# The last stage before attention in a hybrid encoder kernel: another order for the router's product, another buffer for the last q rows, earlier loads of w_out

## The chip, the cores and the metric

The kernel runs on one core of one Trainium2 chip. The metric is the device time of one execution in microseconds (us), median of several runs. Engines are named PE (matmul; PEld is its weight load), DVE, ACT, POOL and SP; SPq and ACTq are the DMA queues that SP and ACT issue on.

## The reference, cut to what matters

Two sequences of 1024 tokens go through one encoder layer: layer norm, a mixer of grouped-query attention and a two-directional RG-LRU, a second layer norm and a hierarchical mixture of experts. Around the change it computes:

```python
proj = h @ w_in                                   # q, k, v, x_lru, y_lru
q = apply_axial_rope(rms_norm(q, q_norm_g), ...)  # the same for k
lru = (h_fwd + h_bwd) * gelu(y_lru)
merged = concatenate([rms_norm(attn, attn_out_g), rms_norm(lru, lru_out_g)])
mix = merged @ w_out
h = layer_norm(DEEPNORM_ALPHA * h + mix, ln1_g, ln1_b)
g_logits = h @ router_wg                          # and e_logits = h @ router_we
```

The kernel reaches the router's logits partly through a product `w_out @ r_w`, where `r_w` holds the 20 columns of `router_wg` and `router_we`. That product needs `w_out` transposed on PE, and it is made in the stage that this case is about.

## The kernel before

`build` calls the stages one after the other: `project_xy`, `qkv_lru`, `attend`, `route`, `experts`, `combine`. Each is a block of its own, and a stage starts when all engines have ended the one before. The change is inside `qkv_lru`.

`qkv_lru` has two interleaved jobs. **Tiles**: for each of 16 tiles of 128 tokens (NT = 16), `front(t)` on PE projects h onto q, k, v and the router's columns with three matmul passes into PSUM tile `pj[t % 2]`; ACT's `square(t)` reads it; DVE and POOL normalise and rotate it; ACT's and POOL's `split(t)` make high and low parts in `q_st` and `k_st`; `back(t, uses)` on PE transposes them into `tr` (uses 0 and 1 are q, use 2 is k); ACT's `evict_q(t)` copies q into the one buffer `q_t`, and `evict_k(t)` issues the store of `q_t` to `q_dram` and copies k. `evict_q(t)` waits until the store of tile t - 1 has landed (`q_stored`). The profile calls `q_t` and its neighbours `wq_raw`, since they lie in that room. **LRU units**: 8 units (NU = 8) of gates, decays, scans and outputs; ACT's `squares_of_output(n)` squares unit n's output and PE's `sums(n, ...)` adds the squares up with matmuls of one column. `GROUPS` gives the order: tile 0, then pairs (1, 2) to (13, 14), then tile 15 alone, which is group g = NU.

The third job is the product with the router's columns. It has UNITS_W = 16 **steps**, and a step n is three things: `turn_w(n)`, four transposes of 128x128 of `w_out` into `gp[n % 2]` (L921); `read_w(n)` on ACT, which copies them to `wo_t[n % 2]` (L1064, shown as `w_out_rows<-gp`); and `times_w(n)`, which multiplies them with `r_w` into `pj[0]` (L930). On PE `times_w(n)` is followed by `turn_w(n + 2)`. `read_w(n)` waits for `turn_w(n)` and `times_w(n - 2)`. After steps 7 and 15 `read_r(half)` copies the product to `lru_th` and `turn_r(half)` transposes it back into `pj[1]`; the last ACT instruction of the stage copies `pj[1]` to `w_r` (shown as `w_out_router<-pj`, L1158).

`w_out` comes in five loads on SP's queue, `WO_LOADS`: rows of 128 numbered (0, 1), (1, 2), (2, 4), (4, 6), (6, 8). The first two, 512 KB each, go to room left by `c_hi` and `c_lo`; the other three, 1024 KB each, go to `wo_late` (shown as `ln_in_g_b`) and are issued once `front(15)` is done.

In the code before, group g = NU places steps 0 to 3 around the transposes of tiles 13 and 14, and then all other steps behind them.

## Time and profile before

| | us |
|---|---|
| median of 3 runs | 1619.41 |
| lowest and highest of them | 1618.01, 1620.03 |
| the profiled execution's own time | 1620.24 |
| its span, first to last instruction | 1618.5 |

The mean granted TensorE clock over the span is 0.956 of full speed, and PE is busy for 90% of it. In what follows times are in us from the start of the span. The stage `qkv_lru` ends near 498.6 and `attend` starts with its first instructions near 499.7. A row of a timeline gives start, duration, engine, line, operation, output and input, the number of instructions merged, and in brackets the idle time before it and what ended it. Rows of matmuls overlap, since matmuls are pipelined: from one row's start to the next is the time that the engine spent on it.

### The profile page before, as it was taken

Reading aid. Unit: us, or ns where it says so; the run is one execution under the profiler, and the core shown is the slowest. Engines: PE = TensorE matmul, PEld = TensorE weight load, DVE = VectorE, ACT = ScalarE, POOL = GpSimd, SP = SyncE. Lnnn points to the kernel's source line nnn. Section 1 sums busy time; section 2 is a strip of 40 time slices with the busy share of each in tenths; the row PEclk is TensorE's granted clock in tenths of the full one; section 3 lists DMA queues with packets and bytes.
Section 4 is the critical chain, followed back from the end, with each engine's and each line's share of the span. In section 5 each row is a group of like instructions: output and inputs, shape, how many; then the busy total and the mean of one; then the engine's idle time right before and its main releaser. Section 6 shows DMA issues by size and latency. Waiting matters only on the chain. (4 is left out here: it accounts for less than half of the span.)

```text
span 1618.5 us, 30220 instructions
## 1 busy us (share of the span) xinstructions
PE 1449.3 (90%) x8946; PEld 1261.0 (78%) x8947; DVE 1125.9 (70%) x2208; ACT 927.7 (57%) x1625; POOL 483.4 (30%) x345
## 2 busy tenths in 40 slices
PE   5999989999976899999999999973999999999940
PEld 5999977777754899999999999972777788777820
DVE  8787548999955888888888888877444333444237
ACT  3444338787855766666666666632555544556325
POOL 1212124575520011111121111122454534544218
PEclk9999999999988999999999999995899999999975
DMA  8865542534444112211112221126798787796576
GB/s 286 303 226 200 211 145 86 189 144 173 165 147 138 61 39 93 72 65 59 59 60 80 76 78 59 47 97 198 233 270 263 182 248 207 200 273 164 104 224 257
DMA packets 126214, 250.09 MB, mean 155 GB/s; under 512 B 24498, under 2 KB 77746, under 8 KB 126132
## 3 DMA queue, kind: packets, MB, share of 16 engines
q1 hardware_dynamic: 94000, 160.97, 28.7%
q0 software_dynamic: 12528, 45.99, 12.3%
q10 hardware_dynamic: 19604, 42.09, 6.8%
q8 instruction: 45, 0.74, 0.2%
q14 instruction: 37, 0.30, 0.1%
HBM read 154.35 MB, written 94.67 MB: 154 GB/s over the span
## 5 line engine op out<-in xcount | busy, mean ns | idle before, releaser
L1736 DVE TENSOR_TENSOR d_probs_t_lo<-d_pt_ps,d_probs_t_hi 128x512 fp32r<-128x512 f32 x256 | 164.9, 686 | 63.4 <-ACT d_probs_t_hi L1650 61.8
L1914 POOL TENSOR_TENSOR d_h_tile<-d_s_tile,d_ln_g_b 128x512 f32<-128x512 f32 x30 | 38.9, 1296 | 532.3 <-ACT d_s_tile L1683 514.6
L1650 ACT ACTIVATE d_probs_t_hi<-d_pt_ps 128x512 fp32r<-128x512 f32 x256 | 139.2, 596 | 95.9 <-PE d_pt_ps L1531 89.5
L1712 DVE TENSOR_REDUCE d_neg_max<-d_s_ps 128x1 f32<-128x1024 f32 x128 | 155.6, 1215 | 3.5 <-PE d_s_ps L1520 3.5
L121 PE MATMUL acc<-k_hi,wl_hi 128*128 128x256 f32 x512 | 145.2, 284 | 4.5 <-DVE k_lo L576 4.5
L121 PE MATMUL e_a_ps<-up_hi,e_xt_hi 128*128 x336 | 136.6, 406 | 10.8 <-issue 5.5
L1633 ACT ACTIVATE d_probs<-d_s_ps,d_neg_max 128x1024 f32<-128x1024 f32 x128 | 143.5, 1121 | 4.2 <-DVE d_neg_max L1712 4.2
L122 PE MATMUL acc<-k_lo,wl_hi 128*128 128x256 f32 x512 | 144.3, 282 | 0.0
L123 PE MATMUL acc<-k_hi,wl_lo 128*128 128x256 f32 x512 | 144.3, 282 | 0.0
L1531 PE MATMUL d_pt_ps<-ident,d_probs 128*128 128x128 f32 x1024 | 132.9, 273 | 4.7 <-ACT d_probs L1633 3.2
L1545 PE MATMUL d_ot_ps<-d_probs_t_hi,d_v_split 128*128 128x256 f32 x512 | 127.4, 287 | 8.3 <-DVE d_probs_t_lo L1736 8.3
L123 PE MATMUL e_a_ps<-up_hi,e_xt_lo 128*128 x336 | 132.5, 394 | 0.0
L122 PE MATMUL e_a_ps<-up_lo,e_xt_hi 128*128 x336 | 132.1, 393 | 0.0
L1545 PE MATMUL d_ot_ps<-d_probs_t_lo,d_v_split 128*128 128x256 f32 x512 | 124.9, 282 | 0.0
L1531 PEld LDWEIGHTS d_pt_ps<-ident,d_probs 128*128 128x128 f32 x1024 | 116.9, 140 | 7.7 <-ACT d_probs L1633 6.5
L121 PE MATMUL d_m_ps<-d_wo_hi,d_m_hi 128*128 128x348 f32 x360 | 120.6, 335 | 0.0
L1519 PE MATMUL d_s_ps<-k_hi,d_q_tile 128*128 128x512 f32 (+1 forms) x256 | 112.0, 438 | 5.7 <-DMA d_q_tile<-q_dram 5.7
L122 PE MATMUL d_m_ps<-d_wo_lo,d_m_hi 128*128 128x348 f32 x360 | 115.8, 322 | 0.0
L123 PE MATMUL d_m_ps<-d_wo_hi,d_m_lo 128*128 128x348 f32 x360 | 115.5, 321 | 0.0
L2391 POOL DMA_INDIRECT e_xg<-h_dram,e_ix x45 | 45.1, 1003 | 231.1 <-ACT e_yt L2518 124.9
L1545 PEld LDWEIGHTS d_ot_ps<-d_probs_t_hi,d_v_split 128*128 128x128 f32 x512 | 97.2, 190 | 15.4 <-issue 15.4
L121 PEld LDWEIGHTS acc<-k_hi,wl_hi 128*128 128x128 f32 x512 | 97.8, 191 | 5.1 <-DVE k_lo L576 5.1
(405 smaller groups left out, 4079.2 us busy)
## 6 DMA issues: line engine op xcount, KB each, us to landing
up_raw<-in_exp_w SPq DMA_DIRECT2D x32, 1024.0 KB, 13.0
down_raw<-in_exp_w SPq DMA_DIRECT2D x16, 1024.0 KB, 13.0
d_h_tile<-h_dram SPq DMA_DIRECT2D x16, 522.0 KB, 4.7
h_dram<-v_all ACTq DMA_DIRECT2D x16, 512.0 KB
ht_hi_dram<-k_hi ACTq DMA_DIRECT2D x8, 1024.0 KB, 4.3
ht_lo_dram<-k_lo ACTq DMA_DIRECT2D x8, 1024.0 KB, 6.7
q_dram<-wq_raw ACTq DMA_DIRECT2D x16, 512.0 KB, 3.0
d_q_tile<-q_dram SPq DMA_DIRECT2D x16, 512.0 KB, 4.2
```

The costliest lines, as they stand in the source:

```text
L121: pe.matmul(out, lhs[0], rhs[0], start=first, stop=False)
L122: pe.matmul(out, lhs[0], rhs[1], start=False, stop=False)
L123: return pe.matmul(out, lhs[1], rhs[0], start=False, stop=last)
L1519: pe.matmul(out, q_t[u][:, h, :], k_hi[:, h // GQ, keys], start=True, stop=False)
L1531: last = pe.transpose(pt_ps[c][:, j, :], pr[h % 2][:, k * P:(k + 1) * P], ident[:])
L1545: last = pe.matmul(ot_ps[:, 0:2 * P], vs[:, s * TPS + k, h // GQ].rearrange("p c d -> p (c d)"), part[:, k].rearrange("p e t -> p (e t)"), ...
L1633: act.activation(pr[h % 2][:], s_ps[h % 2][:], ACT.Exp, bias=nm[:, u, h:h + 1], accum_out=rsum[:, u, h:h + 1]).then_inc(p_done, 1)
L1650: act.activation(pt_hi[:, c * HALF:(c + 1) * HALF, h % 2], pt_ps[c][:], ACT.Copy).then_inc(pth_done[c], 1)
L1712: dve.tensor_reduce(nm[:, u, h:h + 1], s_ps[h % 2][:], AX, ALU.max, negate=True).then_inc(nm_done, 1)
L1736: dve.tensor_tensor(pt_lo[:, part, h % 2], pt_ps[c][:], pt_hi[:, part, h % 2].bitcast(F32), ALU.subtract)\
L1914: pool.tensor_tensor(h1[:, part], s_t[u][:, part], g_b[:, part], ALU.mult).then_inc(hg_done, 1)
L2391: pool.indirect_dma_start(xg[u][:], None, h1_dram, bass.IndirectOffsetOnAxis(ix[u][:, 0:1], 0))\
```

## The change

Steps are placed by number: group NU now holds only `front(15)`, after which PE runs all sixteen steps in a row. Between them come the transposes of tile 13 (q after step 3, k after step 4), of tile 14 (after 6 and 7) and of tile 15 (after 12 and 13), the sums of unit 6 (after step 5, formerly inside `front(15)`) and of unit 7 (after step 14), and `turn_r(0)` after step 9. ACT's list of instructions is rewritten to match. For tile 15 `evict_q` writes to `q_st[0]`, and not to `q_t`, and waits for no store. The load of rows 2 and 3 of `w_out` goes to the gates' weights' room (`gw`, shown as `gate_w`) once the last gate matmul is done; the loads of rows 4 to 7 go ahead of the load of y for unit 7 on SP's queue. The sums of units 6 and 7 are copied by one instruction instead of two.

```diff
--- before.py
+++ after.py
@@ -739,6 +739,7 @@
         tab = both_rt[:, 0:TPS * 2 * HD].rearrange("p (t c d) -> p t c d", t=TPS, c=2)
         q_t = room(NQ * P).bitcast(F32R).rearrange("p (h t) -> p h t", h=NQ)
         q_st = [sb(f"q_st{u}", [P, NQ, 2, HD], F32R) for u in range(2)]
+        q_rows = lambda t: q_t if t < NT - 1 else q_st[NT % 2][:].rearrange("p h c d -> p h (c d)")
 
         gw = sb("gate_w", [P, FT, NG, P])
         ones = sb("ones_b", [P, 2])
@@ -756,7 +757,8 @@
         hr_done = sem("h_router_done")
         hr_stored = sem("h_router_stored")
         wo_early = [c_room[:, n * D:(n + 1) * D] for n in range(4)]
-        wo = wo_early[0::2] + [wo_late[:, k * D:(k + 1) * D] for k in range(KD - 2)]
+        wo_gates = gw[:].rearrange("p f g n -> p (f g n)")
+        wo = wo_early[0::2] + [wo_gates[:, k * D:(k + 1) * D] for k in range(2)] + [wo_late[:, k * D:(k + 1) * D] for k in range(KD - 4)]
         wo_t = wo_early[1::2]
         WO_LOADS = ((0, 1), (1, 2), (2, 4), (4, 6), (6, KD))
         UNITS_W = 2 * KD
@@ -860,14 +862,26 @@
                     load_x(g + 1)
                 if 2 * g + 2 < NT:
                     load_c(2 * g + 2)
-                if g >= NU - 1:
-                    rows = w_out[0].rearrange("(k p) n -> p k n", p=P)
+                rows = w_out[0].rearrange("(k p) n -> p k n", p=P)
+                if g == NU - 1:
                     for n, (a, b) in enumerate(WO_LOADS):
-                        if (b <= 2) != (g == NU - 1):
+                        if b <= 2:
+                            sp.wait_ge(pj_done, NT - 1)
+                            dst = wo[a]
+                        elif b <= 4:
+                            sp.wait_ge(gates_done, GH * NU)
+                            dst = wo_gates[:, (a - 2) * D:(b - 2) * D]
+                        else:
                             continue
-                        sp.wait_ge(pj_done, NT - 1 if b <= 2 else NT)
-                        dst = wo[a] if b <= 2 else wo_late[:, (a - 2) * D:(b - 2) * D]
                         sp.dma_start(dst.rearrange("p (k n) -> p k n", n=D), rows[:, a:b, :]).then_inc(wo_in[n], 16)
+                    store(NU - 2)
+                    sp.wait_ge(pj_done, NT)
+                    for n, (a, b) in enumerate(WO_LOADS):
+                        if a >= 4:
+                            sp.dma_start(wo_late[:, (a - 4) * D:(b - 4) * D].rearrange("p (k n) -> p k n", n=D), rows[:, a:b, :])\
+                              .then_inc(wo_in[n], 16)
+                    load_y(NU - 1)
+                    continue
                 if g == NU:
                     sp.wait_ge(hr_done, NT)
                     with nc.allow_non_contiguous_dma("the router's columns of h's rows"):
@@ -881,11 +895,11 @@
         @block.tensor
         def _(pe):
 
-            def sums(n, out):
+            def sums(n, out, first=SUMS):
                 pe.wait_ge(ones_made, 1)
                 pe.wait_ge(squared, n + 1)
                 for c in range(TPS):
-                    last = pe.matmul(out[:, SUMS + c:SUMS + c + 1], r[n % 2][:, 1, c * P:(c + 1) * P], ones[:, 0:1],
+                    last = pe.matmul(out[:, first + c:first + c + 1], r[n % 2][:, 1, c * P:(c + 1) * P], ones[:, 0:1],
                                      start=True, stop=True)
                 return last
 
@@ -899,9 +913,6 @@
                     for k in range(KD):
                         last = three_pass(pe, pj[u][:, a:b], (c[0][:, k, :], c[1][:, k, :]),
                                           (w_hi[:, k, a:b], w_lo[:, k, a:b]), k == 0, k == KD - 1)
-                if t == NT - 1:
-                    turn_w(0)
-                    turn_w(1)
                 if unit is not None:
                     last = sums(unit, pj[u])
                 last.then_inc(pj_done, 1)
@@ -970,38 +981,33 @@
             for g, group in enumerate(GROUPS):
                 turned = GROUPS[g - 1] if g else []
                 for t in group:
-                    front(t, g - 2 if g >= 2 and t == group[-1] else None)
+                    front(t, g - 2 if 2 <= g < NU and t == group[-1] else None)
                 if g == NU:
-                    for n in range(2):
-                        times_w(n)
-                        turn_w(n + 2)
+                    continue
                 for half in range(2):
                     if half < len(turned):
                         back(turned[half], (0, 1))
-                    if g < NU:
-                        gates(g, 2 * half)
+                    gates(g, 2 * half)
                     if half < len(turned):
                         back(turned[half], (2,))
-                    if g < NU:
-                        gates(g, 2 * half + 1)
-                    if g == NU and half == 0:
-                        times_w(2)
-                        times_w(3)
-            turn_w(4)
-            turn_w(5)
-            for n in range(4, 10):
-                times_w(n)
-                turn_w(n + 2)
-            back(NT - 1, (0, 1, 2))
-            turn_r(0)
-            for n in range(10, 12):
-                times_w(n)
-                turn_w(n + 2)
-            sums(NU - 1, pj[1]).then_inc(last_sums, 1)
-            for n in range(12, UNITS_W):
+                    gates(g, 2 * half + 1)
+            turn_w(0)
+            turn_w(1)
+            for n in range(UNITS_W):
                 times_w(n)
                 if n + 2 < UNITS_W:
                     turn_w(n + 2)
+                if n in (3, 6, 12):
+                    back(NT - 3 + (3, 6, 12).index(n), (0, 1))
+                if n in (4, 7, 13):
+                    back(NT - 3 + (4, 7, 13).index(n), (2,))
+                if n == 5:
+                    pe.wait_ge(v_done, NT)
+                    sums(NU - 2, pj[1]).then_inc(last_sums, 1)
+                if n == 9:
+                    turn_r(0)
+                if n == 14:
+                    sums(NU - 1, pj[1], SUMS + TPS).then_inc(last_sums, 1)
             turn_r(1)
 
         @block.scalar
@@ -1040,16 +1046,16 @@
                    .then_inc(hi_done, 1)
 
             def evict_q(t):
-                if t:
+                if 0 < t < NT - 1:
                     act.wait_ge(q_stored, 16 * t)
                 for part in range(2):
                     use = 3 * t + part
                     act.wait_ge(tr_done, use + 1)
-                    act.activation(q_t[:, 4 * part:4 * part + 4], tr[use % 2][:].bitcast(F32), ACT.Copy).then_inc(tr_free, 1)
+                    act.activation(q_rows(t)[:, 4 * part:4 * part + 4], tr[use % 2][:].bitcast(F32), ACT.Copy).then_inc(tr_free, 1)
 
             def evict_k(t):
                 act.wait_ge(tr_free, 3 * t + 2)
-                act.dma_start(q_dram[TILES[t]], q_t.rearrange("p h t -> p (h t)").bitcast(F32)).then_inc(q_stored, 16)
+                act.dma_start(q_dram[TILES[t]], q_rows(t).rearrange("p h t -> p (h t)").bitcast(F32)).then_inc(q_stored, 16)
                 use = 3 * t + 2
                 act.wait_ge(tr_done, use + 1)
                 cols = slice(TILES[t] * P, (TILES[t] + 1) * P)
@@ -1104,55 +1110,58 @@
             def root(n):
                 act.activation(th[:], th[:], ACT.Sqrt, scale=0.25).then_inc(root_done, 1)
 
-            for g, group in enumerate(GROUPS):
+            for g, group in enumerate(GROUPS[:NU]):
                 turned = GROUPS[g - 1] if g else []
-                if g in (1, NU):
+                if g == 1:
                     split(turned[0])
-                if g == NU:
-                    read_w(0)
-                    read_w(1)
-                square(group[0], g - 2 if g == NU else None)
-                if g < NU:
-                    tanh_table()
+                square(group[0])
+                tanh_table()
                 if len(turned) > 1:
                     split(turned[1])
-                if g == NU:
-                    read_w(2)
-                    read_w(3)
                 if len(group) > 1:
                     square(group[1], g - 2 if g >= 2 else None)
                 for half in range(2):
                     if half < len(turned):
                         evict_q(turned[half])
-                    if g < NU:
-                        gate_tanhs(g, 2 * half)
+                    gate_tanhs(g, 2 * half)
                     if half < len(turned):
                         evict_k(turned[half])
-                    if g < NU:
-                        gate_tanhs(g, 2 * half + 1)
-                if g < NU:
-                    decays(g)
+                    gate_tanhs(g, 2 * half + 1)
+                decays(g)
                 if 0 < g < NU - 1:
                     split(group[0])
-                if g < NU:
-                    root(g)
-                if 0 < g < NU:
+                root(g)
+                if 0 < g < NU - 1:
                     squares_of_output(g - 1)
+            read_w(0)
+            read_w(1)
+            split(NT - 3)
+            square(NT - 1)
+            read_w(2)
+            split(NT - 2)
+            read_w(3)
+            squares_of_output(NU - 2)
             read_w(4)
             read_w(5)
+            evict_q(NT - 3)
+            read_w(6)
+            evict_k(NT - 3)
+            read_w(7)
+            read_w(8)
+            evict_q(NT - 2)
+            read_w(9)
+            evict_k(NT - 2)
+            read_w(10)
+            read_r(0)
             split(NT - 1)
-            for n in range(6, 12):
+            for n in range(11, 15):
                 read_w(n)
-            read_r(0)
             evict_q(NT - 1)
+            read_w(15)
             evict_k(NT - 1)
-            read_w(12)
-            read_w(13)
             squares_of_output(NU - 1)
-            read_w(14)
-            read_w(15)
-            act.wait_ge(last_sums, 1)
-            keep_sums(NU - 1, 1)
+            act.wait_ge(last_sums, 2)
+            act.activation(lru_sums[:, NU - 2:NU, :], pj[1][:, SUMS:SUMS + 2 * TPS].rearrange("p (n c) -> p n c", c=TPS), ACT.Copy)
             read_r(1)
             act.wait_ge(wr_turned, 2)
             act.activation(w_r[:], pj[1][:, 0:KD * RW].rearrange("p (k r) -> p k r", k=KD), ACT.Copy)
```

On PE, from the last matmul of `front(15)`, before the change (L921 is `turn_w`, L888 `sums`, L930 `times_w`, L955 `back`; "x4" are four instructions):

```order
L123 MATMUL pj<-wq_hi,c_lo 128x276
L921 MATMUL gp<-ident,w_out_rows 128x128 x8
L888 MATMUL pj<-ones_b,lru_r 128x1 x8
L930 MATMUL pj<-w_out_rows,logits 20x256 x2
L921 MATMUL gp<-ident,w_out_rows 128x128 x4
L930 MATMUL pj<-w_out_rows,logits 20x256 x2
L921 MATMUL gp<-ident,w_out_rows 128x128 x4
L955 MATMUL tr<-identr,q_st 128x128 x8
L955 MATMUL tr<-identr,k_st 128x128 x4
L930 MATMUL pj<-w_out_rows,logits 20x256 x4
L955 MATMUL tr<-identr,q_st 128x128 x8
L955 MATMUL tr<-identr,k_st 128x128 x4
```

And after the change, from `turn_w(4)`, the first one that reads `gate_w`, to the sums of unit 6 (L932 is `turn_w`, L941 `times_w`, L966 `back`, L902 `sums`):

```order
L932 MATMUL gp<-ident,gate_w 128x128 x4
L941 MATMUL pj<-w_out_rows,logits 20x256 x2
L932 MATMUL gp<-ident,gate_w 128x128 x4
L966 MATMUL tr<-identr,q_st 128x128 x8
L941 MATMUL pj<-w_out_rows,logits 20x256 x2
L932 MATMUL gp<-ident,gate_w 128x128 x4
L966 MATMUL tr<-identr,k_st 128x128 x4
L941 MATMUL pj<-w_out_rows,logits 20x256 x2
L932 MATMUL gp<-ident,gate_w 128x128 x4
L902 MATMUL pj<-ones_b,lru_r 128x1 x8
```

The transposes of tiles 13 and 14 stood together after step 3's transposes; now each half of a tile stands behind a `times_w` and a `turn_w` of its own.

On ACT, the end of the stage before the change (L1048 is `evict_q`, L1052 and the two rows behind it `evict_k`, L1015 `squares_of_output`, L1011 the copy of the sums, L1070 `read_r`):

```order
L1048 ACTIVATE wq_raw<-tr 128x512 x2
L1052 DMA q_dram<-wq_raw 128x1024
L1056 ACTIVATE k_hi<-tr 128x2x128
L1057 ACTIVATE k_lo<-tr 128x2x128
L1064 ACTIVATE w_out_rows<-gp 128x512 x2
L1015 ACTIVATE lru_r<-lru_y 128x1024
L1064 ACTIVATE w_out_rows<-gp 128x512 x2
L1011 ACTIVATE lru_sums<-pj 128x8
L1070 ACTIVATE lru_th<-pj 20x512
L1158 ACTIVATE w_out_router<-pj 128x160
```

And after it (L1054 is `evict_q` of tile 15, which now writes `q_st`, L1070 `read_w`, L1021 `squares_of_output`, L1076 `read_r`):

```order
L1054 ACTIVATE q_st<-tr 128x512 x2
L1070 ACTIVATE w_out_rows<-gp 128x512
L1058 DMA q_dram<-q_st 128x1024
L1062 ACTIVATE k_hi<-tr 128x2x128
L1063 ACTIVATE k_lo<-tr 128x2x128
L1021 ACTIVATE lru_r<-lru_y 128x1024
L1164 ACTIVATE lru_sums<-pj 128x16
L1076 ACTIVATE lru_th<-pj 20x512
L1167 ACTIVATE w_out_router<-pj 128x160
```

The squares of unit 7 stand behind the last `read_w` and the last tile's copies, where two `read_w` stood behind them before.

## Rows read from the trace of the kernel before

**Rows 1.** Stretches of the stage: busy time and count of each engine, PEclk, DMA.

```profile
460.40:473.50 13.10, 5.84 (x29) 3.94 (x28) 10.34 (x11) 3.76 (x8) 3.51 (x5) 0.61 0.68 220
473.50:487.00 13.50, 12.50 (x74) 6.59 (x72) 0.00 (x0) 6.26 (x12) 0.96 (x2) 1.00 0.16 64
```

**Rows 2.** PE's waits, 450.3 to 499: total, times, longest.

```profile
PE tr L955 <- ACT wq_raw L1048: 8.8, 3, 7.3
```

**Rows 3.** PE's timeline over the same stretch.

```profile
450.30 1.03 PE L921 MATMUL gp<-ident,w_out_rows 128*128 128x128 f32 x8
451.59 1.92 PE L888 MATMUL pj<-ones_b,lru_r 128*128 128x1 f32 x16 [0.26 <-ACT lru_r L1015]
453.44 1.04 PE L930 MATMUL pj<-w_out_rows,logits 128*20 128x256 f32 x4
...
468.53 0.72 PE L955 MATMUL tr<-identr,k_st 128*128 128x128 f32 x4 [7.26 <-ACT wq_raw L1048]
469.05 1.93 PE L921 MATMUL gp<-ident,ln_in_g_b 128*128 128x128 f32 x8
470.91 1.90 PE L930 MATMUL pj<-w_out_rows,logits 128*20 128x256 f32 x4
...
473.58 1.04 PE L930 MATMUL pj<-w_out_rows,logits 128*20 128x256 f32 x4
474.55 0.66 PE L921 MATMUL gp<-ident,ln_in_g_b 128*128 128x128 f32 x4
475.14 1.04 PE L930 MATMUL pj<-w_out_rows,logits 128*20 128x256 f32 x4
...
488.79 2.10 PE L888 MATMUL pj<-ones_b,lru_r 128*128 128x1 f32 x16 [1.72 <-ACT lru_r L1015]
490.82 1.89 PE L930 MATMUL pj<-w_out_rows,logits 128*20 128x256 f32 x4
...
494.69 0.66 PE L921 MATMUL gp<-ident,ln_in_g_b 128*128 128x128 f32 x4
...
497.86 0.42 PE L940 MATMUL pj<-ident,lru_th 20*128 20x20 f32 x4 [0.68 <-ACT lru_th L1070]
```

**Rows 4.** ACT's timeline over the same stretch.

```profile
452.18 1.06 ACT L1064 ACTIVATE w_out_rows<-gp 128x512 f32<-128x512 f32 x2
453.54 0.70 ACT L1022 ACTIVATE wq_raw<-pj 128x640 f32<-128x640 f32 x1 [0.31 <-PE pj L888]
...
455.01 0.66 ACT L1038 ACTIVATE q_st<-wq_raw 128x512 fp32r<-128x512 f32 x1
...
455.83 0.63 ACT L1064 ACTIVATE w_out_rows<-gp 128x512 f32<-128x512 f32 x1
...
467.79 1.08 ACT L1048 ACTIVATE wq_raw<-tr 128x512 fp32r<-128x512 f32 x2 [8.25 <-DMA q_dram<-wq_raw]
...
484.19 0.38 ACT L1057 ACTIVATE k_lo<-tr 128x256 fp32r<-128x256 f32 x1
...
487.60 1.05 ACT L1015 ACTIVATE lru_r<-lru_y 128x1024 f32<-128x1024 f32 x1
...
498.31 0.30 ACT L1158 ACTIVATE w_out_router<-pj 128x160 f32<-128x160 f32 x1 [0.51 <-PE pj L940]
```

**Rows 5.** SP's queue, timeline 425 to 515: the DMAs it issues.

```profile
453.54 1.42 SPq L870 DMA_DIRECT2D ln_in_g_b<-in_w_out  x3
455.02 0.88 SPq L874 DMA_DIRECT2D h_dram<-h_router  x1
472.22 0.36 SPq L840 DMA_DIRECT2D lru_dram<-lru_y  x1
```

**Rows 6.** DMA issues with KB each and median us to landing, three stretches: 458 to 459, 468 to 484, 451 to 470.

```profile
q_dram<-wq_raw ACTq DMA_DIRECT2D x1, 512.0 KB, 9.3
...
q_dram<-wq_raw ACTq DMA_DIRECT2D x2, 512.0 KB, 2.6
...
h_dram<-h_router SPq DMA_DIRECT2D x1, 160.0 KB, 15.3
```

**Rows 7.** The three late loads of w_out (tile ln_in_g_b): time to landing.

```profile
DMA to landing us min/median/max: 6.5/9.5/14.4
```

## The prediction

> **What bounds the kernel now.** I first looked at the grouped stretches of the stage, because the page's average (PE busy 90%) says nothing about the 48 us between `front(15)` and the end of the stage. From 460.4 to 473.5 PE is busy for 5.84 of 13.1 us at a granted clock of 0.61, and from 473.5 to 487.0 for 12.5 of 13.5 us at 1.00 [rows 1]. So the same kind of work runs once with PE as the limit and once not. Then PE's waits: 8.8 us for ACT's L1048, `evict_q`, in three waits, of which one holds 7.3 us [rows 2]. Then the timelines. PE stops after tile 14's q transposes until 468.53, idle 7.26 us [rows 3]. ACT stood still at the same time, 8.25 us, and what ended its wait was a DMA, the store of tile 13's q rows [rows 4]. That store took 9.3 us to land, against 2.6 us for the next two [rows 6]. It left in the middle of the three late loads of `w_out`, issued at 453.54, the last of which needed 14.4 us [rows 5, 7]. The bound of the stretch is thus a chain: loads slow the store, the store holds `q_t`, ACT waits with `evict_q(14)`, PE waits with `back(14)`, and steps 4 to 15, though they need none of it, are queued behind on both engines. The stage's last instruction starts on ACT at 498.31 [rows 4].
>
> The chain matters one for one. `attend` begins when the stage has ended, and DVE and SP have long finished: unit 7's output is done by 472.22, when its store is issued [rows 5].
>
> **What PE loses in this stretch.** From 450.30, where the first transposes start, to 497.86, where the last four do, there are 47.6 us [rows 3].
> - Idle: 8.8 us on `evict_q` [rows 2], 0.26 and 1.72 us before the two `sums`, 0.68 us before the last `turn_r` [rows 3]. Sum 11.5.
> - A slow clock. At full clock one `times_w` takes 474.55 - 473.58 = 0.97 us and one `turn_w` 475.14 - 474.55 = 0.59, so a step is 1.56. From 469.05 to 473.58 PE did three `turn_w` and one `times_w` in 4.53 us where 3 x 0.59 + 0.97 = 2.74 would do: 1.8 lost. From 488.79 to 494.69 it did one `sums` (1.85, from 451.59 to 453.44), two `times_w` and one `turn_w` in 5.90, where 4.38 would do: 1.5 lost. Sum 3.3 [rows 3].
>
> Together 14.8 us that are not work at full speed. The work itself, sixteen steps, two sums, three tiles of transposes, two `turn_r`, is the same before and after: the `sums(6)` that leaves `front(15)` comes back after step 5, and one copy of eight columns less is off PE's path.
>
> **What the new order loses instead.** I put the new sequence of both engines side by side from 450.3 on with the durations above. Handing over costs about 0.03 us from a matmul's end to ACT. From ACT's end to PE I take 0.15, an estimate from 497.86, where 0.68 idle contains little but `read_r`. A `read_w` takes 0.6, its successor may start after 0.5 (two take 1.06) [rows 4].
> - Start: `read_w(0)` begins only after `turn_w(0)`, at 450.99, so `times_w(0)` starts at 451.74 where PE is free at 451.48. Idle 0.26.
> - `read_w(2)` stands behind two `read_w`, `split(13)` and `square(15)`. A `split` is 455.83 - 455.01 = 0.82, a `square` 455.01 - 453.54 = 1.47 with the copy of sums that now goes [rows 4]. ACT comes to `read_w(2)` at 454.3, it ends at 454.9, and PE, free at 454.86, starts `times_w(2)` at about 455.1. Idle 0.2.
> - From then on PE gives ACT 1.56 us for each step, and `read_w` needs 0.5 of it. One `split` (0.82), one `squares` (1.05) or one half of `evict_q` (1.08 for two) fits in, the more so as PE has transposes of its own in the same steps. I find no idle time to step 14.
> - `sums(7)` waits for `squares_of_output(7)`, which ACT now reaches only after `read_w(15)` and `evict_k(15)`. After `turn_w(15)` PE has left the k transposes (some 0.4) and `times_w(14)` (0.97), 1.3 us. ACT has 0.03 + 0.5 + two k copies (0.38 each, overlapping, 0.6 to 0.7) + 1.05 + 0.15, that is 2.4 [rows 4]. Idle 1.1.
> - The tail after `times_w(15)` is what it was, 0.68.
>
> Sum 2.2 us. By this schedule `evict_q(14)` starts at 466.6, `turn_w(8)`, the first that needs rows 4 and 5 of `w_out`, at 465.2, and the last ACT instruction near 486.
>
> **The clock.** Before, an idle time of 1.72 us and the `sums` of one column behind it were followed by matmuls at half speed: `times_w` took 1.90 at 490.82 against 1.04 [rows 3]. At 451.59 only 0.26 idle stood before the same `sums`, and the next `times_w` took 1.04. The new 1.1 lies between. I take the worse row: it costs `times_w(15)` 0.85 and the last `turn_r` some 0.15, so 1.0 us. The bound below is nothing.
>
> **DMAs and what they cost.** The load of rows 2 and 3 can go once the gates are done. PE does them ahead of `front(15)`, which ends at 450.3, and `turn_w(4)` needs the rows at 456.0: 5.7 us and the whole length of `front(15)`, where the first late load took 6.5. Rows 4 to 7 leave at about 450.6 instead of 454; with 14.4 us, the longest seen, the last byte is there at 465.0, just before `turn_w(8)` and 8 us before `turn_w(12)` [rows 7]. Store of unit 6 and load of y move behind those issues (about 0.5 us each, three took 1.42 [rows 5]) on SP's queue. y is needed by DVE near 471, and leaves at about 457.6, when `squares_of_output(6)` has run; nothing queued behind it (the router's columns of h, the last LRU store) is read before `attend`. In all 2048 + 512 + 160 KB then leave between 450.6 and 458.5. Before, 3072 + 512 + 512 + 160 = 4256 KB took from 453.54 to 455.02 + 15.3 = 470.3, some 253 KB per us, so they are through at about 461.4 [rows 5, 6]. Tile 13's store leaves at about 461.1, and should land in 2.6 to 4 us. `evict_q(14)` wants it at 466.6, and PE has 0.7 us of slack more: a landing within 6.2 us costs nothing. The other buffer for tile 15 saves nothing by itself, since tile 14's store would have 8 us anyway; I cost it at 0. Its own store leaves near 479.4 and even with 3 us lands before 486.
>
> **Sum.** 14.8 - 2.2 - 1.0 = 11.6 us off 1620.24, the profiled execution's own time: 1608.6. That execution was 0.83 above the median of the runs, so the predicted median is 1619.41 - 11.6 = 1607.8.
>
> **Rivals.**
> *The store still lands late.* y, the router's columns and the ends of `w_out` could still be in flight at 461. For it speaks the 9.3 us [rows 6]; against it that only a sixth as much is outstanding. With 9.3 us it lands at 470.4, `evict_q(14)` begins 3.8 us late and PE loses 3.1. After such a gap the clock would fall as after 468.53, 1.8 more. Gain 11.6 - 4.9 = 6.7: 1612.7.
> *Steps in a row lower the clock, and the kernel is slower.* More than a third of each step is transposes. Should the clock stay at its lower level through them, a step takes 473.58 - 470.91 = 2.67 instead of 1.56, and sixteen cost 17.8 more [rows 3]. The small idle times mostly vanish then, and the result is 1619.41 - 14.8 + 17.8 + 1.5 (sums, tile transposes, tail) = 1623.9. It decides against the change once about 11 of the 16 steps run so. Against it stands the stretch from 473.5 to 487.0, the same mix of steps, at clock 1.00 [rows 1]. The Trainium skill speaks for it: its page "TensorE: Matmul & The Clock Gate", Part 4 (PE-mode transpose), says that transposes don't count as busy for the clock as matmuls do. By that rule alone the time would be this rival's; the trace of this stage doesn't agree, as its clock rose and stayed up with both kinds in turn.
> *The stage's end is set elsewhere, no change.* SP waits for the router's columns of h. They would have to land 25 us later than the 473.4 that issue at about 458 and 15.3 us give [rows 6].
>
> **How the numbers follow.** Chances: forecast 0.78, late store 0.14, slow clock 0.03, no change 0.02, 0.03 for something in between or later. The likeliest case's own range: without a fall of the clock and with `sums` somewhat shorter the gain is 13; another 1 us either way can come from when the clock rises at the start of `attend`, whose first matmuls run after an idle time in both kernels. That gives 1605.5 below. Above, small waits at the many handovers, 0.1 us at each of some 20, and that 1 us give 1610.8. To leave out no more than 2 in 10, the range must take in most of the late store: up to 1612.7. A measurement of this kernel can tell about 0.2%, 3.2 us, from no change. Faster 0.93, within 0.03, slower 0.04.
>
> **What would show it.** Right: no wait of ACT on `q_dram` over 1 us in the stage; PE's idle time between `front(15)` and the last `turn_r` near 2 us, half of it before `sums(7)`; steps 1.56 us apart but where transposes of a tile come between; `w_out_router` at about 486.5; `attend`'s first instructions 1.1 to 1.4 us behind it as before. Wrong: a `turn_w` that waits for a load, an ACT wait before `evict_q(14)`, or PEclk at 0.5 within the steps.

## The result and the profile after

The changed kernel takes 1607.6 us (median of 7 runs, 1603.63 to 1614.01); the kernel before took 1621.95 in 7 runs (1618.01 to 1627.2). The ratio is 0.9908, 95% interval 0.9891 to 0.9926. The predicted median was 1607.8. The profiled execution took 1609.71 with a span of 1607.9, against 1620.24 before.

PE's timeline of the changed kernel, which answers to [rows 3]:

```profile
451.48 1.03 PE L932 MATMUL gp<-ident,w_out_rows 128*128 128x128 f32 x8
452.76 1.04 PE L941 MATMUL pj<-w_out_rows,logits 128*20 128x256 f32 x4 [0.25 <-ACT w_out_rows L1070]
...
455.29 0.66 PE L932 MATMUL gp<-ident,w_out_rows 128*128 128x128 f32 x4
456.00 1.04 PE L941 MATMUL pj<-w_out_rows,logits 128*20 128x256 f32 x4
...
467.99 0.66 PE L932 MATMUL gp<-ident,ln_in_g_b 128*128 128x128 f32 x4
468.40 0.54 PE L966 MATMUL tr<-identr,k_st 128*128 128x128 f32 x4
468.87 1.04 PE L941 MATMUL pj<-w_out_rows,logits 128*20 128x256 f32 x4
469.84 0.66 PE L932 MATMUL gp<-ident,ln_in_g_b 128*128 128x128 f32 x4
470.43 1.04 PE L941 MATMUL pj<-w_out_rows,logits 128*20 128x256 f32 x4
...
481.54 1.92 PE L902 MATMUL pj<-ones_b,lru_r 128*128 128x1 f32 x16 [1.01 <-ACT lru_r L1021]
483.38 1.78 PE L941 MATMUL pj<-w_out_rows,logits 128*20 128x256 f32 x4
485.84 0.61 PE L951 MATMUL pj<-ident,lru_th 20*128 20x20 f32 x4 [0.68 <-ACT lru_th L1076]
```

The 7.26 us before the k transposes of tile 14 are gone: that row, at 468.40, has no bracket. The steps behind it are 1.56 us apart (468.87 to 470.43). The three idle times that are left are 0.25, 1.01 and 0.68; the prediction had 0.26, 1.1 and 0.68, and 0.2 at `times_w(2)`. That one shows no bracket, but `times_w(2)` at 456.00 starts 0.71 us behind `turn_w(3)` where other steps have 0.59, so some 0.1 us of it is there. The kernel before had such a short wait without a bracket too, 0.77 us from a `turn_w` to tile 13's q transposes, where 0.41 would do (467.99 to 468.40 above):

```profile
455.97 0.66 PE L921 MATMUL gp<-ident,w_out_rows 128*128 128x128 f32 x4
456.74 0.88 PE L955 MATMUL tr<-identr,q_st 128*128 128x128 f32 x8
```

The `times_w` at 483.38 takes 1.78 and not 1.04.

Three stretches of the changed kernel, in the columns of [rows 1]:

```profile
451.48:480.50 29.02, 28.72 (x182) 16.93 (x180) 19.66 (x24) 19.16 (x42) 11.06 (x10) 1.00 0.51 157
480.50:483.40 2.90, 1.89 (x18) 1.88 (x18) 0.00 (x0) 0.89 (x1) 0.00 (x0) 1.00 0.31 127
483.40:487.00 3.60, 2.37 (x9) 0.91 (x8) 0.00 (x0) 1.07 (x3) 0.00 (x0) 0.52 0.00 0
```

PE is busy for 28.72 of 29.02 us at a clock of 1.00, through fifteen steps, three tiles' transposes and one `sums`. Only behind `sums(7)` does the clock fall, to 0.52 over the last stretch.

ACT's timeline of the changed kernel around its two critical places ([rows 4] before):

```profile
461.42 0.34 ACTq L1058 DMA_DIRECT2D q_dram<-wq_raw  x1
...
466.99 1.08 ACT L1054 ACTIVATE wq_raw<-tr 128x512 fp32r<-128x512 f32 x2
...
480.06 0.39 ACT L1063 ACTIVATE k_lo<-tr 128x256 fp32r<-128x256 f32 x1
480.32 1.07 ACT L1021 ACTIVATE lru_r<-lru_y 128x1024 f32<-128x1024 f32 x1
...
486.48 0.30 ACT L1167 ACTIVATE w_out_router<-pj 128x160 f32<-128x160 f32 x1 [0.70 <-PE pj L951]
```

Tile 13's store leaves at 461.42. `evict_q(14)` starts at 466.99 without a wait. And its landing, and SP's queue ([rows 5, 6] before):

```profile
lru_y<-y_dram SPq DMA_DIRECT2D x1, 512.0 KB, 4.7
q_dram<-wq_raw ACTq DMA_DIRECT2D x1, 512.0 KB, 5.1
h_dram<-h_router SPq DMA_DIRECT2D x1, 160.0 KB, 6.9
```

```profile
443.07 0.38 SPq L876 DMA_DIRECT2D gate_w<-in_w_out  x1
...
451.67 0.89 SPq L881 DMA_DIRECT2D ln_in_g_b<-in_w_out  x2
458.27 0.34 SPq L838 DMA_DIRECT2D lru_y<-y_dram  x1
458.65 1.21 SPq L888 DMA_DIRECT2D h_dram<-h_router  x1
```

The store took 5.1 us where it had taken 9.3. It landed 0.5 us before `evict_q(14)` wanted it. No load of `w_out` was in flight beside it: the two of rows 4 to 7, issued at 451.67 and 452.1, took 4.9 and 7.0 us and had landed by about 459.1. What was in flight were y (issued at 458.27, 4.7 us, landed at 463.0) and the store of the router's columns of h (458.65, 6.9 us, landed at about 465.6).

In what follows **the stretch** is the time from PE's first `turn_w` behind `front(15)` to the start of ACT's `w_out_router`. It was 498.31 - 450.30 = 48.0 us before and is 486.48 - 451.48 = 35.0 after: 13.0 us less. The two spans differ by 1618.5 - 1607.9 = 10.6. From `w_out_router` to the experts' first matmul it is 636.7 us in both, and `attend`'s first load is issued 1.38 us behind `w_out_router` in both, so what the stretch gained was passed on whole up to there. The rest lies outside the changed code: the stretch began 1.2 us later, the experts' stage was 2.0 us longer and what follows it 0.8 shorter. The experts' stage is taken by the first and last start of one group of its matmuls, first before, then after:

```profile
L121 PE MATMUL e_a_ps<-up_hi,e_xt_hi x336: 389/389/789, 1135.0 to 1541.1; 128*128 x168
```

```profile
L121 PE MATMUL e_a_ps<-up_hi,e_xt_hi x336: 389/389/788, 1123.2 to 1531.3; 128*128 x168
```

That is 406.1 us before and 408.1 after, with the same code. For this reason each experiment below is read by its stretch first, and by its total only where the stretch agrees.

### The profile page after: what moved, and what is told of

Read it like the earlier page. It is cut to its first block and busy times, and to the rows that moved or that the text cites. A ratio compares the mean times of both kernels' runs of the same rounds, so it can differ in the third digit from the quotient of the medians.

```text
span 1607.9 us, 30219 instructions
## 1 busy us (share of the span) xinstructions
PE 1449.5 (90%) x8946; PEld 1261.4 (78%) x8947; DVE 1124.1 (70%) x2208; ACT 928.2 (58%) x1624; POOL 485.2 (30%) x345
## 5 line engine op out<-in xcount | busy, mean ns | idle before, releaser
L1529 PE MATMUL d_s_ps<-k_lo,d_q_tile 128*128 128x512 f32 (+1 forms) x256 | 102.1, 399 | 0.0
```

Of the source, the lines that this page charges most:

```text
L1529: last = pe.matmul(out, q_t[u][:, h, :], k_lo[:, h // GQ, keys], start=False, stop=True)
```

## The experiments

**The changed kernel again**, unchanged, as a yardstick.

> The changed kernel once more, beside the same chip's runs of the kernel before, as the yardstick for the three others. Stretch measured in all of them: from the first transposes of w_out behind front(15) on PE to the start of ACT's last instruction of the stage (w_out_router). It was 48.0 us before (450.30 to 498.31) and 35.0 in the profile after (451.48 to 486.48). Theory (the store's wait is gone and PE is the limit): 35 again, within 0.5, and a total 11 to 15 us below before. Rival (part of the measured 0.9% is a difference between chips): the stretch stays 35 and the total gain comes out clearly below 11.

The stretch was 34.3 us (449.97 to 484.24), ratio 0.9918 (0.9901 to 0.9935). The medians are 13.1 us apart (1622.56 and 1609.47), with both kernels on one chip, so the rival falls. The 0.7 us to 35.0 are the clock. Behind the same idle time and the same sums it stayed up through the last `times_w` this time, and was down only for the last `turn_r` (0.61 us, as in the first profile; 0.42 before):

```profile
480.02 1.92 PE L902 MATMUL pj<-ones_b,lru_r 128*128 128x1 f32 x16 [1.00 <-ACT lru_r L1021]
481.87 1.04 PE L941 MATMUL pj<-w_out_rows,logits 128*20 128x256 f32 x4
483.59 0.61 PE L951 MATMUL pj<-ident,lru_th 20*128 20x20 f32 x4 [0.68 <-ACT lru_th L1076]
```

**The loads alone**, with PE's and ACT's order as before.

```diff
-        wo = wo_early[0::2] + [wo_late[:, k * D:(k + 1) * D] for k in range(KD - 2)]
+        wo = wo_early[0::2] + [wo_gates[:, k * D:(k + 1) * D] for k in range(2)] + [wo_late[:, k * D:(k + 1) * D] for k in range(KD - 4)]
...
+                    store(NU - 2)
+                    sp.wait_ge(pj_done, NT)
```

> The kernel before with the new SP order and the new room for rows 2 and 3 alone; PE and ACT keep the old order. Theory of the store slowed by the loads: 2048 + 512 + 160 KB leave between 450.6 and 455 and are through near 461.4 at 253 KB per us, tile 13's store issued at 458.5 lands in 4 to 5 us and not in 9.3, evict_q(14) starts near 463 instead of 467.8; the stretch falls from 48.0 to 42 to 43.5, a gain of 4.5 to 6. Rival (the loads don't matter to the store; its 9.3 us come from the small rows of the router's columns of h, issued at 455.0): the store still takes 8 us or more, gain under 1.5.

The stretch was 45.9 us (449.95 to 495.90), a gain of 2.1, less than expected; ratio 0.9989 (0.9977 to 1.0002). The store took 6.5 us, so neither side's number held. The expectation had overlooked where `sums(6)` stood:

```profile
451.22 1.92 PE L901 MATMUL pj<-ones_b,lru_r 128*128 128x1 f32 x16 [0.23 <-ACT lru_r L1028]
...
465.36 0.72 PE L968 MATMUL tr<-identr,k_st 128*128 128x128 f32 x4 [4.47 <-ACT wq_raw L1061]
```

```profile
453.17 0.89 SPq L880 DMA_DIRECT2D ln_in_g_b<-in_w_out  x2
454.16 0.41 SPq L837 DMA_DIRECT2D lru_y<-y_dram  x1
454.65 0.62 SPq L887 DMA_DIRECT2D h_dram<-h_router  x1
```

`pj_done` comes behind `sums(6)`, and `sums(6)` behind ACT's squares. So SP issued rows 4 to 7 at 453.17, not at 450. PE's wait fell from 7.26 to 4.47 us. The first two loads landed 4.9 and 7.0 us after their issue, at 458.1 and about 460.6, so the store, issued at 458.13, still met one of them, y and the router's columns.

**The loads, and the sums of unit 6 out of front(15)**.

```diff
-                    front(t, g - 2 if g >= 2 and t == group[-1] else None)
+                    front(t, g - 2 if 2 <= g < NU and t == group[-1] else None)
...
-            sums(NU - 1, pj[1]).then_inc(last_sums, 1)
+            sums(NU - 2, pj[1]).then_inc(last_sums, 1)
+            sums(NU - 1, pj[1], SUMS + TPS).then_inc(last_sums, 1)
```

> The kernel before with the new loads, as in the run of the loads alone, and with the sums of unit 6 taken out of front(15) and put beside those of unit 7, so that pj_done no longer waits 2.6 us behind the squares and sums. In the run of the loads alone SP issued rows 4 to 7 only at 453.2, since pj_done came behind sums(6), and the stretch was 46.0. Theory: the loads leave at 450.3, tile 13's store lands in 4 to 5 us, PE's wait falls from 4.5 to about 3, and sums(6) fills the 1.7 us in which PE waited for the squares of unit 7: stretch 40.5 to 43. Rival (the store's time isn't set by what was issued ahead of it): store over 6 us, stretch 43.5 to 45.

The loads left at 449.00, 0.2 us into the stretch, the store took 5.2 us, and the stretch was 43.5 us (448.81 to 492.35), half a microsecond over the theory's range and at the rival's lower end, though the rival's store of over 6 us didn't come; ratio 0.9976 (0.9959 to 0.9992). Without the sums in front PE came early to things not ready: 1.48 us for the first `read_w` and 0.76 for POOL's part of tile 13. ACT still stood 4.20 us for the store. In the old order only the `times_w` of steps 2 and 3 lie between tiles 13 and 14, so a store that lands in 5.2 us is still too late. The theory had also left out the clock, which fell behind these new waits: the two `times_w` took 3.56 us, where they take 1.90 in the kernel before.

```profile
457.08 3.56 PE L943 MATMUL pj<-w_out_rows,logits 128*20 128x256 f32 x8
```

The two loads, issued at 449.0 and 449.4, had landed by about 456.4 (at most 7.0 us), before the store left at 457.01. So its 5.2 us, like the 5.1 of the changed kernel, are not the loads of `w_out`: y was in flight until about 457.7 and the router's columns (453.04, 7.7 us) until about 460.7.

**The order alone**, with SP's queue and the room for rows 2 and 3 as before.

```diff
-                if g == NU - 1:
+                if g >= NU - 1:
                     for n, (a, b) in enumerate(WO_LOADS):
-                        if b <= 2:
-                            sp.wait_ge(pj_done, NT - 1)
+                        if (b <= 2) != (g == NU - 1):
+                            continue
+                        sp.wait_ge(pj_done, NT - 1 if b <= 2 else NT)
```

> The changed kernel with SP's old order: all three late loads leave only behind the load of y for unit 7, which now waits for squares_of_output(6) near 458.3. Theory (the new order needs rows 2 and 3 at about 457): turn_w(4) waits for a load that leaves at 458.6 and lands 6.5 later, PE idle 8 us, the clock falls (1.8), tile 13's store meets the loads again; the stretch is 45 to 48, a gain of 0 to 3 of 13. Rival (the order of the steps is what brings the gain and the early loads are a detail): stretch under 40.

The stretch was 45.5 us (451.60 to 497.12), a gain of 2.5; ratio 0.9977 (0.9963 to 0.9991). One wait of PE holds it:

```profile
PE gp L919 <- DMA ln_in_g_b<-in_w_out: 8.5, 1, 8.5
```

The rival fell. One point of the theory did too: tile 13's store, now 21 us into the stretch, took 2.6 us and met no wait of ACT.

**All late loads behind front(15), but ahead of y**: the new order, the old room for rows 2 and 3.

```diff
+                        if n == 2:
+                            store(NU - 2)
+                        sp.wait_ge(pj_done, NT - 1 if b <= 2 else NT)
+                        dst = wo[a] if b <= 2 else wo_late[:, (a - 2) * D:(b - 2) * D]
...
+                    load_y(NU - 1)
```

> The changed kernel with all three late loads in their old room, hence after front(15), but ahead of the load of y. In the kernel where they stood behind y, PE waited 8.5 us for rows 2 and 3 and the stretch was 45.5. Theory (what counts is when SP issues the loads, not the gates' room): rows 2 and 3 leave 0.3 us after the stretch begins, land 5.5 to 6.5 later and are wanted 5.5 after the begin, so PE waits 0.3 to 1.5; tile 13's store, issued 10 us after the begin, meets the third load, lands in 5 to 9 and costs PE 0 to 2.5. Stretch 35 to 38. Rival (rows 2 and 3 must come before front(15) ends): PE waits over 4 us and the stretch is over 39.

The stretch was 34.1 us (449.80 to 483.94), 0.2 us under the changed kernel's best, which is what the last `turn_r` gains at full clock (0.42 for 0.61 us); ratio 0.9938 (0.992 to 0.9956). PE waited for no load. The store took 6.3 us and ACT waited for it, but PE did not:

```profile
466.08 1.09 ACT L1044 ACTIVATE wq_raw<-tr 128x512 fp32r<-128x512 f32 x2 [0.67 <-DMA q_dram<-wq_raw]
```

So of "w_out asked for sooner" the part that counts in the stretch is the place in SP's queue, ahead of y; the gates' room isn't needed for it, and the rival falls. The total is a little above the changed kernel's (ratios 0.9908 to 0.9918, intervals that overlap), so a small cost elsewhere isn't excluded. The prediction's threshold, a landing within 6.2 us costs nothing, fits: at 6.3 PE shows no wait. Where the cost begins isn't shown.

**Rows 4 to 7 behind y**: the prediction's first rival, made to happen.

```diff
+                    load_y(NU - 1)
                     sp.wait_ge(pj_done, NT)
                     for n, (a, b) in enumerate(WO_LOADS):
                         if a >= 4:
...
-                    load_y(NU - 1)
```

> The changed kernel with rows 4 to 7 issued behind the load of y, 8.5 us after the stretch begins; rows 2 and 3 stay early. A test of the prediction's first rival and of its threshold (tile 13's store may take 6.2 us without cost). Theory: the store leaves 10 us after the begin amid 2560 KB and takes 5 to 8 us; turn_w(8) wants rows 4 and 5 at 14.3 and they land at 14.5 to 15.5. Stretch 35 to 38. Rival (the loads ahead of the store don't matter once they are not three): store in 2.6 to 4 us, no wait for a load, stretch under 35.

The stretch was 39.5 us (451.60 to 491.10); ratio 0.9952 (0.9936 to 0.9968). PE's rows:

```profile
467.57 0.66 PE L932 MATMUL gp<-ident,ln_in_g_b 128*128 128x128 f32 x4 [1.57 <-DMA ln_in_g_b<-in_w_out]
...
472.22 0.60 PE L966 MATMUL tr<-identr,k_st 128*128 128x128 f32 x4 [1.81 <-ACT wq_raw L1054]
472.75 1.90 PE L941 MATMUL pj<-w_out_rows,logits 128*20 128x256 f32 x4
```

And the store:

```profile
q_dram<-wq_raw ACTq DMA_DIRECT2D x1, 512.0 KB, 9.9
```

Both sides put the store too low; it took 9.9 us, and ACT waited 2.62 us for it. With two loads issued 2.8 and 1.4 us ahead of it, it is as slow as with three issued 5 to 4 us ahead in the kernel before. This run differs from the changed kernel in the place of these two loads alone, so it shows that loads in flight slow the store: 9.9 for 5.1 us. The stretch is 4.5 to 5.2 us longer than the changed kernel's; the prediction had priced this rival at 4.9, by one wait instead of two.

**Tile 14's q rows in another buffer**, in the kernel before.

```diff
+        q_rows = lambda t: q_st[1][:].rearrange("p h c d -> p h (c d)") if t == NT - 2 else q_t
...
-                if t:
+                if 0 < t < NT - 2:
                     act.wait_ge(q_stored, 16 * t)
+                if t == NT - 1:
+                    act.wait_ge(q_stored, 16 * (NT - 2))
...
+                if t == NT - 1:
+                    act.wait_ge(q_stored, 16 * t)
```

> The kernel before, where tile 14's q rows alone go to q_st[1], so that evict_q(14) waits for no store; loads and orders as before; split(15), which writes q_st[1] again, waits for tile 14's store. Theory (the wait for the one buffer held 7.3 us of PE): evict_q(14) starts near 459.5, steps 4 and 5 run at 461, then ACT stands at split(15) until tile 15 is rotated (465.3) or tile 14's store has landed (468 to 470, since it meets the loads too); stretch 40 to 44, gain 4 to 8. Rival (the wait would only be replaced, by the load of rows 2 and 3 and by the store in front of split(15)): stretch over 46, gain under 2.

The rival is right. The stretch was 46.3 us (449.77 to 496.09), a gain of 1.7; ratio 0.9979 (0.9967 to 0.9992). `evict_q(14)` no longer waits for a store, but the wait moved on to `split(15)`, which needs the same buffer free. Tile 14's store, issued at 461.54 amid the loads, took 7.6 us:

```profile
469.25 0.63 ACT L1041 ACTIVATE q_st<-wq_raw 128x512 fp32r<-128x512 f32 x1 [5.69 <-DMA q_dram<-q_st]
```

```profile
470.73 1.89 PE L931 MATMUL pj<-w_out_rows,logits 128*20 128x256 f32 x4 [4.42 <-ACT w_out_rows L1069]
```

**Tile 15's q rows in q_t**, in the changed kernel.

```diff
-        q_rows = lambda t: q_t if t < NT - 1 else q_st[NT % 2][:].rearrange("p h c d -> p h (c d)")
+        q_rows = lambda t: q_t
...
-                if 0 < t < NT - 1:
+                if t:
```

> The changed kernel with tile 15's q rows in q_t like all others, and the wait for tile 14's store. Prediction's costing (the other buffer is worth nothing here): tile 14's store leaves 17 to 18 us after the stretch begins and lands within 3 to 4, evict_q(15) comes 26 us after it: stretch 34.3 to 35.0 as with the buffer. Rival (the buffer is part of the gain): ACT waits on q_dram before evict_q(15) and the stretch is over 36.

The stretch was 34.8 us (448.38 to 483.18) with the clock's fall in it (`times_w` of 1.58 us behind the sums); ratio 0.9922 (0.9902 to 0.9943). ACT waits for no store. In this order the other buffer is worth nothing.

**The squares of unit 7 earlier**, in the changed kernel, beside the changed kernel a third time.

```diff
             for n in range(11, 15):
                 read_w(n)
+                if n == 12:
+                    squares_of_output(NU - 1)
...
-            squares_of_output(NU - 1)
```

> The changed kernel with squares_of_output(7) on ACT moved from behind evict_k(15) to behind read_w(12), where ACT has some 1 us free in each step and unit 7's output has been ready for 2 us. The changed kernel's stretch was 34.1 to 35.0 in four profiles: 34.1 to 34.3 where the clock stayed up behind sums(7), 34.8 to 35.0 where it fell. Theory (PE's 1.0 us before sums(7) is ACT's order alone, and what makes the clock fall in some executions is that idle time with the sums behind it): no wait before sums(7), clock at full level to the end of the products, stretch 33.1 to 33.4. Rival (the squares push read_w(13) and read_w(14) late and PE waits there instead): stretch 33.8 to 34.3.

> The changed kernel a third time, beside the run with the squares moved: stretch 34.1 to 35.0, total 11 to 15 us below the kernel before and 1 to 2 us above the run with the squares moved, a difference that the runs of one chip may not resolve.

The stretch was 33.0 us (449.94 to 482.97), against 34.3 (451.06 to 485.34) for the changed kernel in the same set of runs. Nothing waits before the sums now, and the `times_w` behind them has full speed:

```profile
478.92 1.95 PE L902 MATMUL pj<-ones_b,lru_r 128*128 128x1 f32 x16
480.80 1.04 PE L941 MATMUL pj<-w_out_rows,logits 128*20 128x256 f32 x4
482.51 0.42 PE L951 MATMUL pj<-ident,lru_th 20*128 20x20 f32 x4 [0.68 <-ACT lru_th L1076]
```

Of the 1.3 us, 1.0 is the wait and 0.2 the last `turn_r`, which took 0.62 us in the changed kernel. The part of the theory on the clock is not shown by this: the row at full speed is one profile, and two of the changed kernel's three had their last `times_w` at full speed with the wait in place. (The "four profiles" that the expectation names were two of the changed kernel and two of its variants above.)

Its median is 1605.87 (ratio 0.9905, 0.9887 to 0.9923) and the changed kernel's 1608.25 (0.9914, 0.9895 to 0.9932). The stretch is shorter in the profile; in the totals the two intervals overlap, so that it is faster than the changed kernel isn't shown by them.

## Why the prediction was right

- **The bound.** The chain of loads, store, `q_t`, ACT and PE is shown. The store's time to landing goes with what is in flight beside it: 9.3 us with three loads, 6.5 and 6.3 with the end of one, 9.9 with two issued right ahead of it, and 2.6 for the store of tile 14 in the changed kernel, beside which nothing was left. With the loads of `w_out` landed it was still 5.1 and 5.2, beside y and the router's columns in the one case (y for 1.6 us of it) and mostly the columns in the other (y for 0.7). No run moves the columns' store, so how much of the 9.3 us is theirs isn't shown.
- **The sum.** Forecast for the stretch 11.6 us, measured 13.0 in the profile. Idle times went from 11.5 to 1.9 us (forecast 2.2), and the clock's loss from 3.3 to about 0.9 (1.78 for 1.04 and 0.61 for 0.42). That explains 12.0. In total the profiled execution gained 10.5 and the medians 14.3, with an interval of 12.0 to 17.7 (1621.95 times one minus the ratio's ends); the forecast of 11.6 is just under it. That the predicted median fell so near the measured one owes something to chance: the kernel before stood at 1619.41 in the three runs from which I started, and at 1621.95 in seven.
- **The 1.0 us that the sum missed.** Most of it is in the rows, in what the prediction took for equal. A `turn_w` is passed in 0.41 us where a tile's transposes follow (467.99 to 468.40) and in 0.59 where a `times_w` follows; the new order has six such places, the old one two, one of them with a wait. Against that stand two `times_w` in a row, which the old order had twice and which save 0.1 where nothing waits behind them. Together I make it 0.4. Waits too short for a bracket cost 0.4 before and 0.1 after; before, tile 13's q transposes started 0.77 us behind a `turn_w`, after, `times_w(2)` 0.71 us. Transposes of tiles and `sums` take about 0.1 us longer from start to start where a wait stands beside them, 0.3 in all. And the slow clock before cost 3.5 and not 3.3, since two `turn_w` in a row take 1.03 us [rows 3] and not the 1.18 that the prediction used. These are estimates from differences of starts; they add up to 1.1 us, so nothing clear of rounding stays open. The same 1.18 stands in the prediction's start of `times_w(0)`, 1.44 us into the stretch; it came at 1.28, and that the idle time came out at 0.25 as forecast is chance, since the way over ACT and back was put as much too long as the two `turn_w`.
- **The clock.** Taking the fall behind `sums(7)` as certain was half right: in the three profiles of the changed kernel it struck the last product once (1.78 us for 1.04) and the last `turn_r` each time (0.61 to 0.62 for 0.42). Its price was 0.9 once and 0.2 twice, where the prediction had 1.0.
- **The DMAs.** The store took 5.1 us (4.4 and 4.6 in the two other profiles), above the 2.6 to 4 that the prediction named, and under its threshold of 6.2. The step that failed is the one that has all of 2048 + 512 + 160 KB through at 461.4: it counts 253 KB per us from 450.6 on without a break, but the two loads were through by 459.1, y left only at 458.27 and landed at 463.0, and the router's columns landed at 465.6. It did no harm because 1.1 us of the 6.2 were left.
- **The other buffer at 0**: confirmed.
- **What the prediction did not say** is how the parts share the gain. The loads alone give 2.1 us, the order alone 2.5, both 13.0. The kernel before was profiled once, so gains of this size rest on one pair of profiles each; the ratio's interval leaves 1 out for the order alone and not for the loads alone. Each removes one wait and leaves the next: with early loads the store is still wanted too soon, and with the new order `turn_w(4)` wants rows 2 and 3 some 8.5 us before SP brings them.
- **The rival of a slow clock** is refuted by the changed kernel's first stretch above: 29 us of transposes and products in turn at clock 1.00. The Trainium skill says in "TensorE: Matmul & The Clock Gate", Part 4 (PE-mode transpose), that a transpose doesn't count as busy for the clock the way a matmul does. Taken alone, that did not foretell the time of this mix; how the clock would fare under transposes only, no run here shows.

## What to carry to other kernels

When one engine's in-order queue stands behind a slow store, look at what is queued behind the wait and needs none of it, and spread that work between the waits; the same work then hides the store. Then ask for each load in the new order when it is first wanted and what stands ahead of it on its queue: here the new order without the new queue gave back 10.5 of 13 us. Giving one tile a spare buffer moved the wait to the buffer's next writer.

## What the runs showed that I had not expected

The experts' stage, from the first to the last matmul of one group, took 405.1 to 411.5 us over the twelve profiles of kernels that don't differ there: 406.1 before, 411.2 with the loads alone, 411.5 with tile 14's buffer, 405.1 with the squares earlier, and 406.9 and 410.2 in two profiles of the very same changed kernel. The two profiles of the same kernel are 3.3 us apart, more than the 1.7 to 2.5 us by which some stretches were shorter, so a single total says little about those.

The store of tile 13, 512 KB, took 9.9 us with 2048 KB issued 2.8 and 1.4 us before it, and 6.3 with 3072 KB issued 9.7 to 8.8 us before it. In the second case the last load took 9.3 us and had landed at about 460.2, 0.5 us behind the store's issue, while in the first both were still in flight. So it is not the amount issued that counts but what has not landed yet. Which of the two queues gave way to the other, and why, wasn't tried.
